# Eight-core attention and MLP block: semaphore waits on an engine's own writes, the order around a head's first value products, the place of two scalings, and a bank rotation

## The chip, the cores and the metric

The kernel runs on all eight cores of one Trainium2 chip. Each core handles half of the 128-row tiles of one of the four sequences (the cores of a pair take alternate tiles), and no core waits for another. The metric is the device time of the slowest core, in microseconds (us).

## The reference, cut to what matters

The block works on x of shape (4, 4096, 1024). A first RMS norm feeds one projection to 5120 columns: three 512-column parts of a gated short convolution, q, k and v of four attention heads, and two gates. Per head:

```python
s = einsum('bqhcd,bkhcd->bhcqk', q, k) * scale     # c = 0, 1: two softmax maps per head
s = where(dist >= 0, s - slope[h] * dist, -inf)    # ALiBi, causal
p = softmax(s);  a = p[:, :, 0] - lam * p[:, :, 1]
o = rmsnorm(einsum('bhqk,bkhv->bqhv', a, v), subln_g) * (1 - lam_init)
x = x + (g_a * (conv @ w_a_out) + g_b * (o @ w_b_out)) @ w_o
x = x + square(relu(rmsnorm(x) @ w_mlp_in)) @ w_mlp_out      # then a last rmsnorm
```

## The kernel before, in words

**Order of work.** The program is a list of operations per engine, made in one Python pass; each engine runs its own list strictly in order. `Sched._add` (L62) works out what an operation waits for: the last writers and the readers of the buffers that it names. A wait for TensorE on itself is left out; ScalarE and VectorE do wait, through a semaphore, for their own earlier writer of a buffer (L78 to L81). A write called `part` doesn't wait for earlier `part` writes of the same buffer (L68), and a later reader waits for all of them (L96). Before the change only DMAs could be `part`.

**Stages.** First some 54 us of loads and first projections. Then attention, in four groups `g` of 512 query rows, each of four heads, each head a row of pairs of key tiles (`pairs`, L681 to L686): 4, 8, 12 and 16 pairs per head, 160 in all, numbered n = 0 to 159; group 1 starts at n = 16, group 2 at 48, group 3 at 96. Last, from some 568 us on, the rest of the merge and the MLP.

**One pair.** The main loop (L1285 on) emits for pair n, while n + 1 is prepared:

1. `qk(n + 1)` (L689): four score products, into banks 0 and 1 (s = 0) and 2 and 3 (s = 1). Their left side has 64 rows, so that the two of one s run at the same time.
2. `ex(n + 1)` (L700): the exponentials on ScalarE, PSUM to the tile PT. In heads 1 to 3 it is one instruction per s. In head 0 the ALiBi bias changes at column 256, and there are two per s, both writing the same PT.
3. `work` (L1299): operations put off for later (`run_deferred`, L804: VectorE work in portions, against a credit of 2200 ns a pair), then `one_chunk` (L1238): one chunk, that is one projection of 8 (some 4) products of 512 columns into a free bank, from a list W written out in advance. During pairs this bank is always bank 7, so a chunk waits until the one before it has been copied out (evacuated) by ScalarE or VectorE. Steps of weight 0 in W (loads, statistics) run with the chunk in front of them. Inside, `flush_masks` emits the triangular mask `mask(n + 1)` (L719) on VectorE, for pairs on the diagonal; the first pair of each head is one.
4. `pv(n, 0)` and `pv(n, 1)` (L732): the value products, up to 16 of 129 columns, into banks 4 to 6.

After a head's last pair `epilogue` (L747) copies banks 4 to 6 to SBUF with three VectorE instructions (L752 twice, L755), and queues the rest (L761 to L797) as work for later; then comes one more chunk. So at the start of a head two chunks are apart by no more than `qk` of the next pair: chunk A (from the last iteration of the head before), `qk(n + 1)`, chunk B, then `pv(n, 0)`.

**Group boundaries.** At a group's last pair `until` (L1250) runs all chunks that the next group needs, with banks from a ring: (7, 0, 1, 2, 3), starting at 7. Before group 1 these are the chunk k(1, 3), the small product of `halo_norm` (L557; it takes a bank, weight 0), and four q chunks; before group 2 three v chunks of block 6; before group 3 none. Then follows `qk` of the new group, in banks 0 to 3.

**Statistics.** `stats(blk, ...)` (L501) gives five steps: four Squares on ScalarE (L488, 1024 columns with an accumulator), then `last`: `rstd`, one VectorE operation (L483) and a power on POOL (L484). For blocks 6 and 7 `last` also scales the result on VectorE (L506), which waits for POOL. `halo_stat` (L550) is a Square (L551) with its own root. `spread` (L919) deals the steps out evenly among chunks: W takes `halo_stat`, the five steps for block 1 and two loads among the four chunks `vs(5)`, which run at n = 3 to 6. `halo_chunk` (L613) is copied out by a ScalarE copy (L623) and a VectorE product (L624).

Of the kernel before, what the change touches and what calls it, by code (L numbers as in the profile page):

```python
# [36 lines left out]
class Sched:  # L37
# [66 lines left out]

    def op(self, eng, fn, reads=(), writes=()):
        return self._add(eng, fn, reads, writes, False)

# [123 lines left out]
def build_program():  # L231
# [201 lines left out]

    def act(fn, reads, writes):
        S.op("act", fn, reads, writes)

    def dve(fn, reads, writes):
        S.op("dve", fn, reads, writes)

# [61 lines left out]
    def stats(blk, nxt):  # L501

        def last():
            rstd(rs1[blk], ss1[blk], 4)
            if blk in ksc:
                dve(lambda e: e.tensor_scalar_mul(ksc[blk].ap, rs1[blk].ap, 0.125), [rs1[blk]], [ksc[blk]])  # L506

        def sq(t):
            def f():
                stat_tile(blk, t, tok[(blk, t)])  # L510
                if nxt is not None:
                    tok_load(nxt, t)
            return f
        return [sq(0), sq(1), sq(2), sq(3), last]

# [97 lines left out]
    def halo_chunk(chs):  # L613
        def f():
# [7 lines left out]
            lo, hi = chs[0], chs[-1] + 1  # L622
            act(lambda e: e.copy(hh.ap[:, lo:hi, :], v[:, :, 0, :]), ck, [hh])  # L623
            dve(lambda e: e.tensor_tensor(hh.ap[:, lo:hi, :], v[:, :, 1, :], hh.ap[:, lo:hi, :], ALU.mult),  # L624
# [75 lines left out]
    def ex(n):  # L700
        p = pairs[n]
        g, h, j, cs = p["g"], p["h"], p["j"], p["cs"]
        pts[n] = []
        for s in range(2):
            blk, t = 4 * s + j // 4, j % 4
            PT = pt_ring.next()
            pts[n].append(PT)
            col = ((j - 4 * g + 12) * 2 + s) * 5
            if h == 0:
                parts = [(a, b, col + k) for k, (a, b) in enumerate(((cs, 256), (max(cs, 256), 512))) if a < b]  # L710
            else:
                parts = [(cs, 512, col + 1 + h)]
            scale = ksc[blk].ap[:, t:t + 1] if blk in ksc else 0.125
            for a, b, c in parts:
                act(lambda e, a=a, b=b, c=c, s=s, PT=PT, scale=scale: e.activation(  # L715
                    PT.ap[:, :, a:b], Sb[s][:, :, a:b], AF.Exp, bias=ccol(C_BTAB + c), scale=scale),
                    Sk[s] + [cst] + ([ksc[blk]] if blk in ksc else []), [PT])

# [28 lines left out]
    def epilogue(g, h):  # L747
# [3 lines left out]
        def out(m):  # L751
            dve(lambda e: e.tensor_copy(o[:, m, 0:3, 0:129], bank(4 + m)[:, 0:390].rearrange(  # L752
                "p (t e) -> p t e", t=3)[:, :, 0:129]), [pk(4 + m)], [o_raw])
        out(0)
        dve(lambda e: e.tensor_copy(o[:, :, 3, 0:129], bank(6)[:, 0:260].rearrange(  # L755
            "p (m e) -> p m e", m=2)[:, :, 0:129]), [pk(6)], [o_raw])
        out(1)
# [429 lines left out]
    mark(0)  # L1187
    W += [(0, f) for f in normed(0)] + spread(ks(5)[1:], [])
    W += spread(vs(5), [halo_stat] + stats(1, 2) + wc_load(0))
    W += spread(vs(1), xT_steps(2, 2))  # L1190
# [58 lines left out]

    def until(name, banks=range(8)):  # L1250
        keep, oring[0] = oring[0], Ring(list(banks))
        while pos[0] < marks[name]:
            one_chunk(marks[name])
# [31 lines left out]
    for n, p in enumerate(pairs):  # L1285
        if n == n_a3 - 16:
            g_loads2(0)
        if n + 1 < len(pairs):
            if pairs[n + 1]["g"] != p["g"]:
                until(pairs[n + 1]["g"], (7, 0, 1, 2, 3))  # L1290
            qk(n + 1)
# [7 lines left out]
        def work(room):  # L1299
# [3 lines left out]
            one_chunk(limit)  # L1303
            flush_masks()
        if not p["last"]:
            work(2200 - (400 if diag else 0))
        pv(n, 0)
        pv(n, 1)
# [159 lines left out]
```

How the kernel before makes its waits and increments, by code:

```python
        def run(e, eng):  # L135
            seen = {}
            for i, o in enumerate(self.ops[e]):
                deps = set(o["deps"])
                if o["is_dma"]:
                    j = o["ev"][2]
                    if j >= N_DMA_SEMS:
                        deps.add(("d", e, j - N_DMA_SEMS))
                need = {}
                for d in deps:
                    s, v = sem_val(d)
                    if need.get(id(s), (s, 0))[1] < v:
                        need[id(s)] = (s, v)
                for key, (s, v) in sorted(need.items(), key=lambda kv: kv[1][1]):
                    if seen.get(key, 0) >= v:
                        continue
                    seen[key] = v
                    eng.wait_ge(s, v)
                ins = o["fn"](eng)
                if o["is_dma"]:
                    s, v = sem_val(o["ev"])
                    ins.then_inc(s, 16)
                elif i in cval[e]:
                    ins.then_inc(csem[e], 1)
            n = self.dma_count[e]
            for k in [(n + q) % N_DMA_SEMS for q in range(N_DMA_SEMS)]:
                cnt = (n - k + N_DMA_SEMS - 1) // N_DMA_SEMS if n > k else 0
                if cnt > 0:
                    eng.wait_ge(dsem[e][k], 16 * cnt)
```

## Time and profile before

| | us |
|---|---|
| median of 3 runs (lowest, highest) | 1164.12 (1163.68, 1166.56) |
| profiled execution, its own time | 1163.79 |
| its span on the slowest core (core 5) | 1162.2 |
| spans of the eight cores | 1160.2 to 1162.2 |
| granted TensorE clock, mean, of the cores | 0.995 to 0.998 |
| TensorE busy | 1127.2 (97% of the span) |
| ScalarE busy / VectorE busy | 550.3 / 466.9 |

PE is TensorE, PEld its loads of weights, ACT ScalarE, DVE VectorE, POOL GpSimd. All matrix products have line L441, so they are told apart by form and by time. The record of one product lasts from its start to its result in PSUM, while the next starts long before that; "busy" is the union of the records, and "idle before" counts only what no record covers. In the rows below, "<-" names what ended a wait.

### The profile page before, as it was taken

Reading aid. Unit: us, or ns where it says so; the run is one execution under the profiler, and the core shown is the slowest. Engines: PE = TensorE matmul, PEld = TensorE weight load, DVE = VectorE, ACT = ScalarE, POOL = GpSimd, SP = SyncE. Lnnn points to the kernel's source line nnn. Section 1 sums busy time; section 2 is a strip of 40 time slices with the busy share of each in tenths; the row PEclk is TensorE's granted clock in tenths of the full one; section 3 lists DMA queues with packets and bytes.
Section 4 is the critical chain, followed back from the end, with each engine's and each line's share of the span. In section 5 each row is a group of like instructions: output and inputs, shape, how many; then the busy total and the mean of one; then the engine's idle time right before and its main releaser. Section 6 shows DMA issues by size and latency. Waiting matters only on the chain.

```text
span 1162.2 us, 20430 instructions; the slowest of 8 cores (1160.2 to 1162.2 us)
## 1 busy us (share of the span) xinstructions
PE 1127.2 (97%) x7162; PEld 563.0 (48%) x7162; DVE 466.9 (40%) x1051; ACT 550.3 (47%) x760; POOL 84.3 (7%) x136
## 2 busy tenths in 40 slices
PE   7999999999999999999999999999999999999997
PEld 3444555455455555555544444444444444444444
DVE  2476666644654632433435544222221322223212
ACT  2585786676666888878523223321231033003301
POOL 5212001001001001001100001000000000000000
PEclk8999999999999999999999999999999999999999
DMA  9877522332067059375296686911210140012001
GB/s 140 166 144 138 144 90 51 110 56 46 5 132 147 19 99 179 65 191 105 38 253 168 207 165 172 158 43 55 70 57 1 55 111 17 19 55 73 2 37 55
DMA packets 67491, 111.46 MB, mean 96 GB/s; under 512 B 37216, under 2 KB 40288, under 8 KB 66368
## 3 DMA queue, kind: packets, MB, share of 16 engines
q0 software_dynamic: 15056, 40.22, 22.5%
q1 hardware_dynamic: 52192, 69.68, 20.0%
q8 instruction: 60, 0.98, 0.4%
q14 instruction: 39, 0.32, 0.1%
q10 hardware_dynamic: 144, 0.26, 0.1%
HBM read 114.40 MB, written 29.36 MB: 124 GB/s over the span
## 4 chain that ended last, share of the span: by engine, by line
PE 92%; ACT 3%; DVE 2%; issue 2%; DMA 1%; POOL 0%; DVEq 0%; ACTq 0%; POOLq 0%
PE ps_all L441 92%; ACT big L715 2%; DMA big<-wv 1%; DVE big L780 0%; DVE big L594 0%; DVE big L604 0%; POOL big L484 0%; ACT big L852 0%; DVE big L772 0%; DVE big L863 0%; DVE big L574 0%; ACT big L592 0%; POOL big L446 0%; DVEq L152 0%; DVE big L571 0%
## 5 line engine op out<-in xcount | busy, mean ns | idle before, releaser
L441 PE MATMUL ps_all<-big 128*128 128x512 bf16 (+7 forms) x7162 | 1127.2, 323 | 28.9 <-ACT big L715 8.2
L441 PEld LDWEIGHTS ps_all<-big 128*128 128x128 bf16 (+2 forms) x7162 | 563.0, 98 | 592.9 <-issue 100.7
L715 ACT ACTIVATE big<-ps_all,big 128x1024 bf16<-128x1024 f32 (+3 forms) x384 | 338.3, 926 | 111.4 <-PE ps_all L441 104.4
L982 ACT ACTIVATE big<-ps_all 128x512 bf16<-128x512 f32 x128 | 76.5, 598 | 137.6 <-PE ps_all L441 137.4
L983 DVE TENSOR_TENSOR big<-big 128x512 bf16<-128x512 bf16 x128 | 54.5, 426 | 156.5 <-ACT big L982 156.0
L999 ACT ACTIVATE big<-big 128x1024 bf16<-128x1024 f32 x15 | 15.9, 1057 | 187.9 <-DVE big L994 187.9
L863 DVE SCALAR_TENSOR_TENSOR big<-big,ps_all 128x512 f32<-128x512 f32 x64 | 43.7, 687 | 106.3 <-PE ps_all L441 106.3
L994 DVE SCALAR_TENSOR_TENSOR big<-ps_all,big 128x512 f32<-128x512 f32 x30 | 22.5, 752 | 143.5 <-PE ps_all L441 143.5
L852 ACT ACTIVATE big<-ps_all,big 128x512 f32<-128x512 f32 x64 | 43.6, 686 | 67.7 <-PE ps_all L441 66.6
L898 ACT ACTIVATE big<-big 128x1024 bf16<-128x1024 f32 x16 | 16.9, 1057 | 47.0 <-DVE big L893 47.0
L724 DVE TENSOR_TENSOR big<-big 128x256 bf16<-128x256 bf16 x64 | 18.5, 289 | 46.7 <-ACT big L715 46.6
L893 DVE SCALAR_TENSOR_TENSOR big<-ps_all,big 128x512 f32<-128x512 f32 x32 | 22.1, 691 | 29.2 <-PE ps_all L441 29.0
L788 POOL TENSOR_TENSOR big<-big 128x4 f32<-128x4 f32 x16 | 17.4, 1088 | 158.4 <-DVE big L786 153.6
L772 DVE SCALAR_TENSOR_TENSOR big<-big 128x128 f32<-128x128 f32 x64 | 22.4, 351 | 5.5
L867 DVE TENSOR_TENSOR big<-big 128x512 bf16<-128x512 f32 x32 | 22.2, 692 | 3.7 <-DVE big L863 0.5
L594 DVE TENSOR_SCALAR big<-ps_all,big 128x512 bf16<-128x512 f32 x18 | 13.5, 751 | 24.1 <-PE ps_all L441 24.1
L534 DVE SCALAR_TENSOR_TENSOR big<-big 128x512 bf16<-128x512 bf16 x32 | 22.7, 745 | 0.0
L446 POOL DMA_DIRECT2D big<-xT x33 | 18.4, 586 | 46.5 <-PE ps_all L441 46.4
L780 DVE SCALAR_TENSOR_TENSOR big<-big 128x128 f32<-128x128 f32 x64 | 18.7, 292 | 7.2 <-DVE big L780 0.5
L488 ACT ACTIVATE big<-big 128x1024 bf16<-128x1024 f32 x20 | 21.1, 1057 | 0.5
L752 DVE COPY big<-ps_all 128x387 f32<-128x387 f32 x32 | 17.9, 560 | 4.2 <-PE ps_all L441 2.5
L1102 ACT ACTIVATE big<-big 128x512 bf16<-128x512 bf16 x24 | 13.4, 621 | 12.4 <-DMA big<-xT 12.4
(90 smaller groups left out, 296.8 us busy)
## 6 DMA issues: line engine op xcount, KB each, us to landing
big<-xs SPq DMA_DIRECT2D x36, 512.0 KB, 6.8
big<-w POOLq DMA_DIRECT2D x32, 512.0 KB, 8.1
xm_sp<-big SPq DMA_DIRECT2D x16, 512.0 KB, 3.8
big<-xm_sp SPq DMA_DIRECT2D x16, 512.0 KB, 5.8
big<-xT POOLq DMA_DIRECT2D x31, 256.0 KB, 7.6
out<-big SPq DMA_DIRECT2D x15, 512.0 KB, 2.7
xn_sp<-big SPq DMA_DIRECT2D x4, 1024.0 KB, 6.6
big<-wg POOLq DMA_DIRECT2D x8, 512.0 KB, 5.9
```

What stands on the lines that cost most here:

```text
L441: S.op("pe", lambda e: e.matmul(out, lhsT, rhs, start=start, stop=stop, skip_group_check=skip), reads, writes)
L488: act(lambda e: e.activation(junk.ap, xt.ap, AF.Square, accum_out=ss1[blk].ap[:, t:t + 1]), [xt], [junk, ss1[blk]])
L534: dve(lambda e: e.scalar_tensor_tensor(x[k].ap, x[k].ap, ccol(C_GMIX + k), r.ap, ALU.mult, ALU.mult), [x[k], cst, r], [x[k]])
L715: act(lambda e, a=a, b=b, c=c, s=s, PT=PT, scale=scale: e.activation(PT.ap[:, :, a:b], Sb[s][:, :, a:b], AF.Exp, bias=ccol(C_BTAB + c), sc ...
L772: dve(lambda e, t=t: e.scalar_tensor_tensor(o[:, 0, t, 0:128], o[:, 0, t, 0:128], rl[:, 0, t:t + 1], o[:, 1, t, 0:128], ALU.mult, ALU.add) ...
L852: lambda ps, lo, hi, key: act(lambda e: e.activation(t.ap[:, lo:hi], ps, AF.Tanh, bias=hbg.ap[:, 8 * w + dm:8 * w + dm + 1], scale=0.5), k ...
L863: lambda ps, lo, hi, key: dve(lambda e: e.scalar_tensor_tensor(t.ap[:, lo:hi], t.ap[:, lo:hi], 1.0, ps, ALU.add, ALU.mult), key + [t], [t]))
L867: dve(lambda e: e.tensor_tensor(g_m[dm].ap, a.ap, b.ap, ALU.add), [a, b], [g_m[dm]])
L893: dve(lambda e: e.scalar_tensor_tensor(x.ap[:, o:o + 512], ps, 0.5, x.ap[:, o:o + 512], ALU.mult, ALU.add), key + [x], [x])
L982: act(lambda e: e.activation(r.ap, ps, AF.Relu), key, [r])
L983: dve(lambda e: e.tensor_tensor(h2[fc].ap, r.ap, r.ap, ALU.mult), [r], [h2[fc]])
L994: dve(lambda e: e.scalar_tensor_tensor(x.ap[:, hs], ps, r2q[b].ap[:, t:t + 1], x.ap[:, hs], ALU.mult, ALU.add), key + [x, r2q[b]], [x])
```

## The change

- `op`, `act` and `dve` get the argument `part`. The exponentials of one PT tile, and the three copies of `epilogue` into `o_raw`, become parts: the second and third no longer wait for the one before on their own engine. The mask and other readers wait for all.
- `stats` gives the scaling of blocks 6 and 7 as a sixth step of its own, `scaled`, so that `spread` deals out six steps.
- `halo_chunk`'s copy moves from ScalarE to VectorE.
- In W, the three chunks `ks(5)[1:]` and the four `vs(5)` now share the five statistics steps of block 1, `halo_stat` and the two loads, in this order.
- `until` for groups 1 to 3 takes its banks from (0, 1, 2, 3, 7), and the ring's start is set to minus the sum of the weights that are left, modulo five.
- At the first pair of every head but the very first, `pv(n, 0)` goes ahead of the chunk, and `pv(n, 1)` stays behind it.

```diff
--- before.py
+++ after.py
@@ -102,8 +102,8 @@
             self.readers.setdefault(k, []).append(ev)
         return ev
 
-    def op(self, eng, fn, reads=(), writes=()):
-        return self._add(eng, fn, reads, writes, False)
+    def op(self, eng, fn, reads=(), writes=(), part=False):
+        return self._add(eng, fn, reads, writes, False, (), part)
 
     def dma(self, eng, fn, reads=(), writes=(), extra=(), part=False):
         return self._add(eng, fn, reads, writes, True, extra, part)
@@ -431,11 +431,11 @@
             late_masks.pop(0)()
 
 
-    def act(fn, reads, writes):
-        S.op("act", fn, reads, writes)
-
-    def dve(fn, reads, writes):
-        S.op("dve", fn, reads, writes)
+    def act(fn, reads, writes, part=False):
+        S.op("act", fn, reads, writes, part)
+
+    def dve(fn, reads, writes, part=False):
+        S.op("dve", fn, reads, writes, part)
 
     def mm(out, lhsT, rhs, start, stop, reads, writes, skip=False):
         S.op("pe", lambda e: e.matmul(out, lhsT, rhs, start=start, stop=stop, skip_group_check=skip),
@@ -502,8 +502,9 @@
 
         def last():
             rstd(rs1[blk], ss1[blk], 4)
-            if blk in ksc:
-                dve(lambda e: e.tensor_scalar_mul(ksc[blk].ap, rs1[blk].ap, 0.125), [rs1[blk]], [ksc[blk]])
+
+        def scaled():
+            dve(lambda e: e.tensor_scalar_mul(ksc[blk].ap, rs1[blk].ap, 0.125), [rs1[blk]], [ksc[blk]])
 
         def sq(t):
             def f():
@@ -511,7 +512,7 @@
                 if nxt is not None:
                     tok_load(nxt, t)
             return f
-        return [sq(0), sq(1), sq(2), sq(3), last]
+        return [sq(0), sq(1), sq(2), sq(3), last] + ([scaled] if blk in ksc else [])
 
     def bcast(blk):
 
@@ -620,7 +621,7 @@
                            xnTh.ap[:, c, :], c == 0 and w == 0 and q == 0, c == 7, [Wc[ch], xnTh], ck, skip=True)
             v = pc[:, 0:64 * len(chs)].rearrange("p (q w t) -> p q w t", w=2, t=32)
             lo, hi = chs[0], chs[-1] + 1
-            act(lambda e: e.copy(hh.ap[:, lo:hi, :], v[:, :, 0, :]), ck, [hh])
+            dve(lambda e: e.tensor_copy(hh.ap[:, lo:hi, :], v[:, :, 0, :]), ck, [hh])
             dve(lambda e: e.tensor_tensor(hh.ap[:, lo:hi, :], v[:, :, 1, :], hh.ap[:, lo:hi, :], ALU.mult),
                 ck + [hh], [hh])
         return f
@@ -711,10 +712,11 @@
             else:
                 parts = [(cs, 512, col + 1 + h)]
             scale = ksc[blk].ap[:, t:t + 1] if blk in ksc else 0.125
+            S.parts.discard(PT)
             for a, b, c in parts:
                 act(lambda e, a=a, b=b, c=c, s=s, PT=PT, scale=scale: e.activation(
                     PT.ap[:, :, a:b], Sb[s][:, :, a:b], AF.Exp, bias=ccol(C_BTAB + c), scale=scale),
-                    Sk[s] + [cst] + ([ksc[blk]] if blk in ksc else []), [PT])
+                    Sk[s] + [cst] + ([ksc[blk]] if blk in ksc else []), [PT], True)
 
     def mask(n):
         p = pairs[n]
@@ -750,10 +752,11 @@
 
         def out(m):
             dve(lambda e: e.tensor_copy(o[:, m, 0:3, 0:129], bank(4 + m)[:, 0:390].rearrange(
-                "p (t e) -> p t e", t=3)[:, :, 0:129]), [pk(4 + m)], [o_raw])
+                "p (t e) -> p t e", t=3)[:, :, 0:129]), [pk(4 + m)], [o_raw], True)
+        S.parts.discard(o_raw)
         out(0)
         dve(lambda e: e.tensor_copy(o[:, :, 3, 0:129], bank(6)[:, 0:260].rearrange(
-            "p (m e) -> p m e", m=2)[:, :, 0:129]), [pk(6)], [o_raw])
+            "p (m e) -> p m e", m=2)[:, :, 0:129]), [pk(6)], [o_raw], True)
         out(1)
         rl = est.ap[:, 0:8].rearrange("p (m t) -> p m t", m=2)
 
@@ -1185,8 +1188,8 @@
     W = []
     W += [(0, f) for f in xT_steps(1, 0)] + [(1, ks(5)[0])]
     mark(0)
-    W += [(0, f) for f in normed(0)] + spread(ks(5)[1:], [])
-    W += spread(vs(5), [halo_stat] + stats(1, 2) + wc_load(0))
+    W += [(0, f) for f in normed(0)]
+    W += spread(ks(5)[1:] + vs(5), stats(1, 2) + [halo_stat] + wc_load(0))
     W += spread(vs(1), xT_steps(2, 2))
     W += [(1, bcast(1))]
     W += spread(ks(1) + qs(1), stats(2, None) + wc_load(1) + [halo_norm]
@@ -1247,8 +1250,10 @@
             pos[0] += 1
         return w
 
-    def until(name, banks=range(8)):
+    def until(name, banks=range(8), turn=False):
         keep, oring[0] = oring[0], Ring(list(banks))
+        if turn:
+            oring[0].i = -sum(w for w, f in W[pos[0]:marks[name]]) % len(banks)
         while pos[0] < marks[name]:
             one_chunk(marks[name])
             run_deferred(900)
@@ -1287,7 +1292,7 @@
             g_loads2(0)
         if n + 1 < len(pairs):
             if pairs[n + 1]["g"] != p["g"]:
-                until(pairs[n + 1]["g"], (7, 0, 1, 2, 3))
+                until(pairs[n + 1]["g"], (0, 1, 2, 3, 7), True)
             qk(n + 1)
             ex(n + 1)
             if pairs[n + 1]["first"]:
@@ -1302,9 +1307,13 @@
                 late_masks.append(lambda: mask(n + 1))
             one_chunk(limit)
             flush_masks()
+        lead = p["first"] and n > 0
+        if lead:
+            pv(n, 0)
         if not p["last"]:
             work(2200 - (400 if diag else 0))
-        pv(n, 0)
+        if not lead:
+            pv(n, 0)
         pv(n, 1)
         if p["last"]:
             epilogue(g, p["h"])
```

## Rows read from the trace of the kernel before

**Rows 1.** Windows, middle and last stage: TensorE, weight loads, VectorE, ScalarE, GpSimd busy.

```profile
54.05:567.95 513.90, 492.36 (x4114) 270.36 (x4115) 261.93 (x631) 388.31 (x480) 54.09 (x78) 1.00 0.48 99
...
567.95:1162.20 594.25, 588.17 (x2756) 269.55 (x2756) 186.91 (x372) 140.67 (x244) 11.66 (x21) 1.00 0.35 88
```

**Rows 2.** Groups by form, TensorE: count, busy us, mean ns of one record.

```profile
L441 PE MATMUL ps_all<-big 128*128 128x512 bf16 x4064 | 907.5, 380 | 14.8 <-DMA big<-xT 2.1 <-DVE big L566 2.0 <-DVE big L571 1.8
L441 PE MATMUL ps_all<-big 128*128 128x129 bf16 x2176 | 149.4, 220 | 0.7 <-DVE big L724 0.7
```

**Rows 3.** Chain of waits, last stage: start, us, what.

```profile
567.95 588.18 PE ps_all L441 x2756
```

**Rows 4.** Timeline of ScalarE, head 0 of group 2.

```profile
244.24 3.01 ACT L715 ACTIVATE big<-ps_all,big 128x512 bf16<-128x512 f32 x4 [0.38 <-PE ps_all L441]
...
254.35 1.36 ACT L715 ACTIVATE big<-ps_all,big 128x512 bf16<-128x512 f32 x2 [0.80 <-PE ps_all L441]
```

**Rows 5.** Chain of waits, first pairs of group 1, head 0.

```profile
114.44 0.79 ACT big L715
...
115.37 0.71 PE ps_all L441 x3
```

**Rows 6.** Windows: pairs 98 to 105, 62 to 69, 50 to 56, 106 to 109.

```profile
382.00:409.55 27.55, 27.14 (x228) 15.20 (x226) 14.30 (x33) 23.91 (x35) 1.83 (x2) 1.00 0.12 27
266.05:292.16 26.11, 26.11 (x226) 14.43 (x225) 8.66 (x21) 19.46 (x20) 3.23 (x5) 1.00 0.32 46
226.36:250.40 24.04, 23.84 (x198) 13.39 (x196) 11.87 (x28) 21.19 (x31) 2.37 (x4) 1.00 0.21 40
409.55:422.64 13.09, 11.73 (x106) 6.87 (x106) 2.36 (x4) 12.29 (x20) 1.05 (x2) 1.00 0.55 97
```

**Rows 7.** Timeline of TensorE at the two group boundaries.

```profile
102.53 12.38 PE L441 MATMUL ps_all<-big 128*128 128x512 bf16 x60 [0.49 <-DVE big L483]
...
213.19 5.66 PE L441 MATMUL ps_all<-big 128*128 128x512 bf16 x25 [0.55 <-DVE big L594]
219.54 2.97 PE L441 MATMUL ps_all<-big 64*128 64x512 bf16 x17 [0.69 <-DVE big L483]
```

**Rows 8.** Timeline of VectorE around the two L506.

```profile
176.28 0.17 DVE L506 TENSOR_SCALAR big<-big 128x4 f32<-128x4 f32 x1 [1.46 <-POOL big L484]
...
302.44 0.17 DVE L506 TENSOR_SCALAR big<-big 128x4 f32<-128x4 f32 x1 [1.29 <-POOL big L484]
```

**Rows 9.** Timeline of TensorE behind them.

```profile
179.62 2.57 PE L441 MATMUL ps_all<-big 128*128 128x512 bf16 x20 [1.12 <-DVE big L604]
...
305.55 3.33 PE L441 MATMUL ps_all<-big 128*128 128x512 bf16 x28 [1.01 <-DVE big L571]
```

**Rows 10.** Timeline of ScalarE, pairs 4 and 5.

```profile
67.29 1.04 ACT L551 ACTIVATE big<-big 32x1024 bf16<-32x1024 f32 x1
...
69.57 1.85 ACT L715 ACTIVATE big<-ps_all,big 128x768 bf16<-128x768 f32 x2
```

**Rows 11.** Timeline of TensorE, pairs 5 and 6.

```profile
72.14 2.57 PE L441 MATMUL ps_all<-big 128*128 128x512 bf16 x20 [0.29 <-ACT big L592]
...
75.76 0.23 PE L441 MATMUL ps_all<-big 64*128 64x128 bf16 x2 [0.44 <-ACT big L715]
```

**Rows 12.** Timeline of TensorE, start of group 1, head 3 (pair 40).

```profile
191.40 2.79 PE L441 MATMUL ps_all<-big 128*128 128x512 bf16 x24 [0.34 <-DVE big L761]
```

**Rows 13.** Timeline of VectorE at the same place.

```profile
189.65 0.56 DVE L752 COPY big<-ps_all 128x387 f32<-128x387 f32 x1
190.12 0.28 DVE L724 TENSOR_TENSOR big<-big 128x256 bf16<-128x256 bf16 x1
```

**Rows 14.** Timelines: VectorE at pair 17, TensorE at pair 59.

```profile
121.69 0.75 DVE L594 TENSOR_SCALAR big<-ps_all,big 128x512 bf16<-128x512 f32 x1
...
259.89 0.39 PE L441 MATMUL ps_all<-big 128*128 128x129 bf16 x4 [0.66 <-DVE big L724]
260.50 2.42 PE L441 MATMUL ps_all<-big 128*128 128x512 bf16 x12 [0.21 <-DVE big L525]
```

## The prediction

> **What bounds the kernel now.** I read the windows by stage first. In the last stage TensorE is busy for 588.17 of 594.25 us, and the chain of waits calls all of it one run of products; in the middle stage, from 54 to 568 us, it is busy for 492.36 of 513.90 [rows 1, 3]. The change touches only operations of the middle stage and the bank rings in front of it, so the last stage moves as a block, and the question is how much of the middle stage's waiting goes away.
>
> Idle time understates that waiting. The long run has 2756 products in 588.18 us, 0.213 us from start to start, while the record of a 512-column product lasts 0.380 [rows 2, 3]. So a product's record covers 0.165 us of any gap behind it (a value product's 0.220 record does the same: four in 0.39 us start 0.057 apart [rows 14]); behind a pair of score products, which start together, the whole 0.380 is covered where the second of the pair is late, and, by my estimate, 0.07 where a chunk follows, since it can't start at once in any case. I give each stall from start to start: idle plus that cover. The middle stage's 21.5 us idle sit in some 45 gaps, so about 29 us can be won at most, 21.5 + 45 x 0.165.
>
> **Exponentials.** Head 0 has 40 pairs, of which 32 have two exponentials per s, so 64 instructions lose their wait. Four in a row with two such waits take 3.01 us, two without one take 1.36; as one record is about 0.77, a step without a wait is 0.59 [rows 4]. Two more such steps on the 1.36 would give 2.54, so the waits cost at most 0.47 in four; scaled by a tile's column rather than by a constant an instruction is slower by some 0.09, which leaves 0.29 as the least. I take 0.19 a wait, 0.37 a pair. That is 11.9 us of ScalarE, but it counts only where TensorE waits for it:
> - In groups 1, 2 and 3 the chain runs through the first pair's exponentials to the score product that needs their bank again (pair 17's, 115.37) [rows 5]: 3 x 0.37 = 1.1. A like stall at pair 21 gives 0.4.
> - Eight pairs of group 3's head 0 took 27.55 us, eight of group 2's head 1, which have one exponential per s, 26.11, 3.26 a pair: 1.44 lost. Seven of group 2's head 0 took 24.04 against 22.85: 1.19 lost [rows 6]. Each pair's excess, 0.17, is under the 0.37 that ScalarE gets back, so nearly all goes; I take 1.2 and 1.0.
> - Pairs 106 to 109, where gates are on ScalarE too, took 13.09 us for 106 products and had 1.36 idle [rows 6]. Four pairs' 0.37 is 1.5; pairs with a chunk of four stay bound by ScalarE: 1.1.
>
> Together **4.8**. Bounds: 0 (ScalarE gets nothing back) and 6.3 (all these stalls end).
>
> **Banks.** Before group 1 the chunk k(1, 3) waited 0.49 + 0.165 = 0.66 us for bank 7, which the chunk before had just filled; before group 2 the first v chunk waited 0.55 + 0.165 = 0.72 in the same way, and then the second score product waited for bank 1, the last chunk's, 0.69 + 0.38 = 1.07 [rows 7]. With the new ring group 2's three chunks get banks 2, 3 and 7: -1.79, banks 2 and 3 being free since pair 47's small exponentials. For group 1 the weights left are k and four q, sum 5, modulo 5 nothing; but `halo_norm` also takes a bank, with weight 0. So six banks are drawn: 0, 1, 2, 3, 7, and 0 for the last q chunk, right before `qk(16)` wants bank 0. Before, the same six draws from (7, 0, 1, 2, 3) ended on 7. There the k chunk's 0.66 goes, and the wait that group 2 loses, 1.07, comes. So 1.79 + 0.66 - 1.07 = **1.4** is won. Bounds: 0.8 if the first chunks wait for exponentials in their new banks, 2.4 if no stall comes at group 1.
>
> **Roots.** L506 held VectorE for 1.46 us at block 6 and 1.29 at block 7, waiting for POOL's power; behind it stood the conv operations and the copy of bank 7, and TensorE waited 1.12 + 0.07 and 1.01 + 0.07 us [rows 8, 9]. As a step of its own the scaling comes two chunks later for block 6 and one for block 7, over 3 us, and finds POOL done. -1.19 in full; at block 7 VectorE has 2.2 us of the epilogue's work queued in front of the copy, so -0.9: **2.1**. The price is that Squares move up by a chunk; one lands before pair 28's exponentials, where TensorE waits for them: 0.27 later. Bounds 1.2 to 2.7.
>
> **Order in W, halo copy.** Between exponentials of pairs 4 and 5 ScalarE ran L551 and a Square, 2.3 us (67.29 to 69.57) [rows 10], then two more Squares before pair 6's. TensorE waited at each bank they shared: four stalls, of which two are shown, 0.37 and 0.60 by start, 1.9 in all; and 0.45 more at pair 4, 0.13 at pair 6 [rows 11]. In the new order Squares run at pairs 0 to 3, where ScalarE has time, and only one of them stands before pair 5. Left is the copy of a v chunk behind pair 5's exponentials, 0.34, and the next copy behind VectorE's epilogue work, some 0.4. So 2.5 - 0.75 = 1.75. The halo copy on VectorE frees a 0.24 wait at pair 28, which the 0.27 above takes back. **1.6**. Bounds 0.8 and 2.5.
>
> **A head's first value products.** Chunk B waits for bank 7 from chunk A, 0.34 + 0.07 = 0.42 us at pair 40 [rows 12]; the eight value products put between last 8 x 0.057 = 0.46 and cover it. They need the head's mask: it ended at 190.40, chunk B started at 191.40 [rows 12, 13], and the copies lose their own waits, so the products find it done. What is late next is chunk B itself: it is copied out 0.46 later in relation to chunk C. With 0.43 us to spare there, where VectorE is prompt, that costs 0.03. But where VectorE works its queue without a pause, as at pair 17, whose copy started with no idle before it [rows 14], the 0.46 comes back as a stall. By heads: stalls of 0.37 to 0.48 at pairs 8, 32, 40, 60, 72, 84, 144 (2.9) and of 0.16 at 48, 112 and 128 (0.5) go; given back are 0.46 at 12, 0.44 at 16, 0.36 at 40, 0.42 at 144 (ScalarE is late there whatever comes), 0.22 at 8, and small ones, together 2.0. **1.4**. Bounds: -1.5 and 3.4.
>
> **Own waits of VectorE's copies.** Two consecutive copies without a wait overlap: the mask started 0.09 before the second L752 ended (190.12 against 190.21), while a waited one starts some 0.1 after [rows 13]. So some 0.2 to 0.4 us of VectorE a head, off the path except as room for the mask: nothing.
>
> The Trainium skill (VectorE: DVE Perf Modes, "The DRAIN you can't avoid") says that chained operations can't save by dropping semaphores, since the next one doesn't start until the pipe is empty, and that the semaphore costs nothing extra. By that rule the copies gain nothing, which doesn't touch the sum; taken for ScalarE as well it would take 4.8 out. The rows show an overlap where no wait stands, on both engines, so the measurement decides against it here.
>
> **Sum.** 4.8 + 1.4 + 2.1 + 1.6 + 1.4 = 11.3. The profiled execution's own time is 1163.79, 0.33 under the median of the runs, so 1163.79 - 11.3 = **1152.5**.
>
> **Rivals.**
> 1. *The waits cost nothing, or the change doesn't take them away* (another buffer of the same instruction still orders them). For: the span of an instruction hardly tells pipe from wait. Against: rows 4. The 4.8 is gone: 1157.3. Chance 0.08.
> 2. *VectorE's queue eats the head starts.* Each start gives back 0.25 us instead of gaining: 1152.5 + 1.4 + 15 x 0.25 = 1157.7. For: pair 17. Against: most evacuations had idle time before them. Chance 0.1.
> 3. *The ring is right in every group*, if the small product's bank is free early or its draw doesn't count: 1152.5 - 1.07 = 1151.4. Chance 0.12.
> 4. *Slower.* TensorE is in order, so a value product that stands before the chunk blocks it. If VectorE's queue makes the mask late, as at pair 59, where the products waited 0.66 + 0.07 us and the chunk behind them 0.21 + 0.165 more [rows 14], each of 15 starts stalls by these 1.1. It decides from (11.3 - 1.4) / 15 = 0.66 us a start; at 1.1 the time is 1163.8 - 9.9 + 16.5 = 1170.4. Against: 1.0 us in hand at pair 40. Chance 0.03.
> 5. *1 and 2 together*: 1162.5, no change. Chance 0.05.
>
> The forecast has 0.62. About 0.3% (3.5 us) is what a measurement can tell from no change. **Range** 1148.5 to 1158.0: it holds rivals 1 to 3; the lower end is 4 us of the 6 that the upper bounds allow beyond the sum, the upper one leaves out 4, 5 and the lowest bounds taken together. Faster by over 0.3%: 0.91; within: 0.06; slower: 0.03.
>
> **What would show it.** Second exponentials start 0.1 before the one before ends, and eight pairs of head 0 take some 26.3 us. At group 1 a score product waits about 1 us for the copy of a q chunk, at group 2 none. L506 has no idle before it. At heads' first pairs value products come right behind the scores, without idle before them, and stalls of chunk C or D show at pairs 12, 16 and 40. The middle stage takes 502.6 us instead of 513.9; the last stage is unchanged. Wrong would be: a longer last stage, head 0 at its old pace, or idle time before first value products.

## The result, and the profile after

The changed kernel took 1150.99 us (median of 4 runs) against 1164.05 for the kernel before: a ratio of 0.9882, interval 0.9863 to 0.9902, some 13 us faster. One of its four runs took 1224.45 us, with the cores of one die at a lower granted clock (0.915 to 0.939), and all ratios here leave such runs out. The forecast was 1152.5, range 1148.5 to 1158.0. The profiled execution's own time is 1150.69, its span 1149.1 us on core 7.

The time went where it was looked for. Windows by stage, changed kernel (columns as in [rows 1]):

```profile
53.32:554.38 501.06, 488.65 (x4114) 268.61 (x4115) 259.75 (x633) 381.67 (x477) 53.65 (x78) 1.00 0.52 102
554.38:1149.10 594.72, 588.33 (x2756) 269.50 (x2756) 186.62 (x372) 140.43 (x244) 11.65 (x21) 1.00 0.34 88
```

The middle stage went from 513.90 us [rows 1] to 501.06, that is 12.8 less (502.6 had been forecast), and TensorE's idle time in it from 21.5 to 12.4. The last stage, forecast unchanged, is 0.47 us longer on this core. The chain of waits shows one new break in what was a single piece [rows 3]:

```profile
554.38 45.28 PE ps_all L441 x209
...
599.71 0.19 ACT big L901
599.90 0.58 ACT big L855
...
600.62 542.43 PE ps_all L441 x2544
```

A gate's activation by ScalarE (L855), which empties a bank, came behind the accumulator read of a Square (L901). The forecast's "unchanged" holds on three of the six cores whose product records are complete (594.20 to 594.28 us) and misses by 0.3 to 0.7 on the other three, while all six of the kernel before lie at 594.23 to 594.27. Whether the break belongs to the change isn't shown.

**Exponentials.** Windows of pairs 98 to 105, 62 to 69, 50 to 56 and 106 to 109 (answering to [rows 6]):

```profile
370.63:396.95 26.32, 26.29 (x227) 14.73 (x226) 14.70 (x34) 22.49 (x35) 1.83 (x2) 1.00 0.14 26
257.11:283.22 26.11, 26.11 (x226) 14.43 (x224) 9.08 (x22) 20.50 (x22) 3.23 (x5) 1.00 0.37 47
219.22:242.26 23.04, 23.01 (x198) 13.03 (x197) 12.38 (x29) 19.89 (x32) 2.42 (x4) 1.00 0.23 41
396.95:409.01 12.06, 11.60 (x106) 6.65 (x104) 2.36 (x4) 11.49 (x19) 1.05 (x2) 1.00 0.64 104
```

Eight pairs of head 0 take 26.32 us (27.55 before; "some 26.3 us" forecast) and keep up with a head that has one exponential per s, which is as it was at 26.11; seven pairs take 23.04 (24.04), and the four with gates 12.06 (13.09). ScalarE's timeline at the same head as [rows 4]:

```profile
236.22 2.60 ACT L717 ACTIVATE big<-ps_all,big 128x512 bf16<-128x512 f32 x4 [0.67 <-PE ps_all L441]
...
245.86 1.36 ACT L717 ACTIVATE big<-ps_all,big 128x512 bf16<-128x512 f32 x2 [0.96 <-PE ps_all L441]
```

Four exponentials take 2.60 us instead of 3.01, so a wait on the own engine cost 0.205 (0.19 was taken), and two that never had one still take 1.36. ScalarE now waits 0.67 us for TensorE before that row (0.38 before the change), and TensorE has no more than 0.03 us idle in the eight pairs.

**Group boundaries.** TensorE at groups 1 and 2 (answering to [rows 7]), and VectorE before group 1:

```profile
109.58 2.99 PE L441 MATMUL ps_all<-big 64*128 64x512 bf16 x18 [0.95 <-DVE big L605]
112.83 3.46 PE L441 MATMUL ps_all<-big 64*128 64x512 bf16 x28 [0.27 <-ACT big L717]
...
211.72 7.46 PE L441 MATMUL ps_all<-big 128*128 128x512 bf16 x47
```

```profile
108.74 0.69 DVE L605 TENSOR_TENSOR big<-ps_all,big 128x512 bf16<-128x512 f32 x1 [0.38 <-PE ps_all L441]
```

Before group 2 nothing waits any more. Before group 1 the score product of pair 16 waits 0.95 us idle for L605, the copy of the last q chunk: the weight-0 draw of `halo_norm` has put it into bank 0, as forecast ("about 1 us").

**Roots and head starts.** VectorE's two scalings, then TensorE around pairs 36 and 40 and VectorE at pair 40 (answering to [rows 8, 9, 12, 13]):

```profile
171.36 0.16 DVE L507 TENSOR_SCALAR big<-big 128x4 f32<-128x4 f32 x1
...
292.05 0.16 DVE L507 TENSOR_SCALAR big<-big 128x4 f32<-128x4 f32 x1
```

```profile
167.78 8.40 PE L441 MATMUL ps_all<-big 128*128 128x129 bf16 x69
...
183.87 8.35 PE L441 MATMUL ps_all<-big 128*128 128x129 bf16 x61
```

```profile
185.19 0.28 DVE L726 TENSOR_TENSOR big<-big 128x256 bf16<-128x256 bf16 x1
```

Neither scaling has idle time before it, and at the two places where TensorE waited 1.12 and 0.34 us it now runs through. The mask of pair 40 ended at 185.47, in the middle of that run, before its value products.

**What is left.** TensorE's stalls behind head starts:

```profile
97.22 2.99 PE L441 MATMUL ps_all<-big 128*128 128x512 bf16 x19 [0.66 <-DVE big L575]
120.50 2.68 PE L441 MATMUL ps_all<-big 128*128 128x512 bf16 x22 [0.65 <-DVE big L595]
299.08 1.24 PE L441 MATMUL ps_all<-big 128*128 128x512 bf16 x5 [0.59 <-DVE big L572]
```

These are stalls of a later chunk, such as the prediction expected at heads 12, 16 and 40, where VectorE works its queue without a pause: chunks 14 and 18 wait, the one expected behind head 40 doesn't, and chunk 74, behind head 72, does.

### The profile page after: what moved, and what is told of

It reads as the page before. It is cut to its first block, busy times and chain, and to the rows that moved or that the text cites. A ratio compares the mean times of both kernels' runs of the same rounds, so it can differ in the third digit from the quotient of the medians.

```text
span 1149.1 us, 20398 instructions; the slowest of 8 cores (1147.2 to 1149.1 us)
## 1 busy us (share of the span) xinstructions
PE 1122.7 (98%) x7162; PEld 560.4 (49%) x7162; DVE 464.4 (40%) x1053; ACT 544.2 (47%) x758; POOL 83.8 (7%) x136
## 4 chain that ended last, share of the span: by engine, by line
PE 93%; ACT 2%; DVE 1%; DMA 1%; issue 1%; POOL 0%; DVEq 0%; ACTq 0%; POOLq 0%
PE ps_all L441 93%; ACT big L717 1%; DMA big<-wv 1%; POOL big L446 0%; DVE big L783 0%; DVE big L866 0%; DVE big L775 0%; ACT big L593 0%; DVE big L605 0%; DVE big L575 0%; ACT big L855 0%; DVE big L595 0%; DVE big L758 0%; DVE big L572 0%; DVE big L731 0%
## 5 line engine op out<-in xcount | busy, mean ns | idle before, releaser
L717 ACT ACTIVATE big<-ps_all,big 128x1024 bf16<-128x1024 f32 (+3 forms) x384 | 331.7, 927 | 103.5 <-PE ps_all L441 102.1
L866 DVE SCALAR_TENSOR_TENSOR big<-big,ps_all 128x512 f32<-128x512 f32 x64 | 43.7, 686 | 106.2 <-PE ps_all L441 106.0
L855 ACT ACTIVATE big<-ps_all,big 128x512 f32<-128x512 f32 x64 | 43.6, 686 | 68.0 <-PE ps_all L441 65.7
L901 ACT ACTIVATE big<-big 128x1024 bf16<-128x1024 f32 x16 | 16.9, 1057 | 47.9 <-DVE big L896 47.9
L726 DVE TENSOR_TENSOR big<-big 128x256 bf16<-128x256 bf16 x64 | 18.4, 288 | 44.4 <-ACT big L717 44.3
L791 POOL TENSOR_TENSOR big<-big 128x4 f32<-128x4 f32 x16 | 17.4, 1088 | 135.1 <-DVE big L789 130.9
L446 POOL DMA_DIRECT2D big<-xT x33 | 18.5, 596 | 43.9 <-PE ps_all L441 43.8
L1063 DVE SCALAR_TENSOR_TENSOR big<-big 128x1024 f32<-128x1024 f32 x15 | 19.1, 1276 | 0.0
```

The costliest lines, as they stand in the source:

```text
L855: lambda ps, lo, hi, key: act(lambda e: e.activation(t.ap[:, lo:hi], ps, AF.Tanh, bias=hbg.ap[:, 8 * w + dm:8 * w + dm + 1], scale=0.5), k ...
L866: lambda ps, lo, hi, key: dve(lambda e: e.scalar_tensor_tensor(t.ap[:, lo:hi], t.ap[:, lo:hi], 1.0, ps, ALU.add, ALU.mult), key + [t], [t]))
```

## The experiments

From here on the middle stage is the measure: the time from its first product to the first of the last stage, on core 7 of each profiled execution. (Two of the eight cores lack some records of products and are left out throughout.) Over the six cores of two executions of the changed kernel it lies between 500.69 and 501.23, while the stage ahead of it took 52.2 to 55.5 us without regard to the kernel. "By the starts of the score products" means: the score products come in the same order in every kernel, so the start of each, counted from the stage's first product, is set against its start in the other kernel, and where the difference jumps the time was lost or won. A jump at pair n + 2 belongs to chunk n or the products beside it. The ratio is that of the timed runs.

| kernel | middle stage, us | against its base | ratio to before (interval) |
|---|---|---|---|
| before | 513.92 | | |
| changed | 501.06 | -12.86 | 0.9882 (0.9863, 0.9902) |
| changed, again | 501.05 | -12.87 | 0.9892 (0.9875, 0.9909) |
| without exponentials' part | 506.98 | +5.92 | 0.9942 (0.9924, 0.9959) |
| before + exponentials' part | 508.90 | -5.02 | 0.9958 (0.9943, 0.9973) |
| without roots | 503.44 | +2.38 | 0.9906 (0.9888, 0.9924) |
| without order and halo copy | 503.65 | +2.59 | 0.9914 (0.9890, 0.9938) |
| old ring | 502.15 | +1.09 | 0.9898 (0.9880, 0.9916) |
| without head starts | 502.17 | +1.11 | 0.9902 (0.9886, 0.9918) |
| before + head starts | 513.11 | -0.81 | 0.9991 (0.9981, 1.0000) |
| copies wait again | 501.33 | +0.27 | 0.9889 (0.9872, 0.9907) |
| ring of six at group 1 | 499.82 | -1.24 | 0.9875 (0.9851, 0.9899) |
| the same, no head start at 12, 16 | 499.22 | -1.84 | 0.9879 (0.9862, 0.9896) |
| ring of six, less room | 501.67 | +0.61 | 0.9887 (0.9869, 0.9905) |

One thing must be taken off first. The cores of the changed kernel differ in two places above all: 0.16 us at pair 122 and 0.11 at pair 125. In its first execution cores 1, 3, 5 and 7 have both and take 501.06 to 501.23; in both executions the cores with neither take 500.69 to 500.81. No row says what these two stalls wait for. Core 7 of the first execution, the base of the third column, has both. On core 7 of the other rows only "changed, again" and the last have one, the 0.16. So, like with like, the whole change is worth 13.1, each undone part 0.27 more than the column says, and the ring of six 0.27 less.

**1. Exponentials, undone and alone.** First the changed kernel with the exponentials waiting again:

```diff
-                    Sk[s] + [cst] + (...), [PT], True)
+                    Sk[s] + [cst] + (...), [PT])
```

> The changed kernel, but the exponentials of a tile wait for their own engine again. My theory: the 0.19 us a wait come back on ScalarE and the 4.8 us of the sum come back, 1151.0 + 4.8 = 1155.8; from pair 98's to pair 106's first score product the time goes from some 26.4 us to 27.5, the stall of pair 49's score product grows by 0.37. Rival 1 (a wait for the own engine costs nothing): 1151.0, with the pace of the changed kernel. Rival 2 (the gain lies in the order around a head's start): 1151.0 as well.

Then the kernel before with only that part:

> The kernel before with the exponentials' change alone. My theory: 4.8 us less, 1159.2, less what the second wait at the same place takes back: pair 18's chunk waits for VectorE at the same moment as for ScalarE, so pair 19's 0.35 stays. Rival 1: 1164.0. If the gain needs the other parts: 1162 to 1163.

The windows of pairs 98 to 105 (first without the part in the changed kernel, then with it in the kernel before):

```profile
374.93:402.76 27.83, 27.15 (x226) 15.20 (x226) 14.71 (x34) 23.91 (x35) 1.83 (x2) 1.00 0.10 22
```

```profile
380.70:407.01 26.31, 26.27 (x226) 14.71 (x225) 14.39 (x33) 22.49 (x35) 1.83 (x2) 1.00 0.14 27
```

ScalarE's 1.42 us in eight pairs (23.91 less 22.49) come and go with the waits, and the eight pairs get longer or shorter by as much: 1.51 in the changed kernel, 1.24 in the one before. Rival 1 is out. Alone the part is worth 5.0, in company 6.2 (5.9 and the 0.27): by the starts of the score products, 0.3 of the difference lies at pairs 17 to 20 and 0.27 in pairs 98 to 105, where TensorE waited longer for ScalarE once other waits were gone, and 0.28 each at pairs 29 and 149. Those two are in heads with one exponential per s, which the edit doesn't touch; at 29 a score product waits for ScalarE, but why it is later there stays open.

**2. Roots, undone.**

```diff
             rstd(rs1[blk], ss1[blk], 4)
+            if blk in ksc:
+                scaled()
...
-        return [sq(0), sq(1), sq(2), sq(3), last] + ([scaled] if blk in ksc else [])
+        return [sq(0), sq(1), sq(2), sq(3), last]
```

> The changed kernel with the scaling by 1/8 of the roots of blocks 6 and 7 again in the step of the root itself, so that VectorE waits for POOL there. My theory: 2.1 us come back, 1153.1: L506's wait of some 1.3 to 1.5 us on VectorE returns twice, and with it TensorE's 1.19 at pair 36 and 0.9 at pairs 73 and 74. Rival (other work fills the place, as TensorE's own time is the bound): 1151.0 with the wait on VectorE but no stall on TensorE.

TensorE at pairs 36 and 73, roots undone:

```profile
177.65 4.52 PE L441 MATMUL ps_all<-big 128*128 128x512 bf16 x34 [0.93 <-DVE big L607]
...
299.11 3.33 PE L441 MATMUL ps_all<-big 128*128 128x512 bf16 x28 [1.41 <-DVE big L574]
```

Both stalls are back, 0.99 and 1.46 us by the starts of the score products, with 0.17 more at pair 35. Between the kernel before and the changed one the same two places gave 1.17 and 1.06.

**3. Order in W and halo copy, undone.**

```diff
-            dve(lambda e: e.tensor_copy(hh.ap[:, lo:hi, :], v[:, :, 0, :]), ck, [hh])
+            act(lambda e: e.copy(hh.ap[:, lo:hi, :], v[:, :, 0, :]), ck, [hh])
...
-    W += [(0, f) for f in normed(0)]
-    W += spread(ks(5)[1:] + vs(5), stats(1, 2) + [halo_stat] + wc_load(0))
+    W += [(0, f) for f in normed(0)] + spread(ks(5)[1:], [])
+    W += spread(vs(5), [halo_stat] + stats(1, 2) + wc_load(0))
```

> The changed kernel with the old order of the statistics among the chunks of block 5 and the halo copy on ScalarE again. My theory: 1.6 us come back; the four stalls at pairs 5 to 7 (0.47, 0.37, 0.45, 0.60) return, less what the products ahead of the chunk cover, and 0.24 at pairs 24 and 28. Rival (ScalarE has room enough once the rest is changed): no difference.

TensorE at pairs 5 and 6, then at pairs 24 and 28, both undone (core 5):

```profile
72.01 0.28 PE L441 MATMUL ps_all<-big 64*128 64x256 bf16 x2 [0.60 <-ACT big L717]
72.59 2.57 PE L441 MATMUL ps_all<-big 128*128 128x512 bf16 x20 [0.29 <-ACT big L593]
75.53 0.23 PE L441 MATMUL ps_all<-big 64*128 64x128 bf16 x2 [0.38 <-ACT big L717]
76.20 0.23 PE L441 MATMUL ps_all<-big 64*128 64x128 bf16 x2 [0.43 <-ACT big L717]
...
141.94 11.98 PE L441 MATMUL ps_all<-big 128*128 128x129 bf16 x134 [0.30 <-DVE big L764]
154.69 1.67 PE L441 MATMUL ps_all<-big 128*128 128x512 bf16 x7 [0.16 <-DVE big L625]
```

The changed kernel has at pairs 5 to 7 one stall of 0.15 (the v chunk's copy behind pair 5's exponentials) and one of 0.30, and at pairs 24 and 28 neither of the other two. There the halo copy (L624), behind the exponentials on ScalarE, held VectorE's product with it (L625). VectorE before the first of the two (core 5):

```profile
141.37 0.23 DVE L625 TENSOR_TENSOR big<-ps_all,big 128x64 f32<-128x64 f32 x1 [1.06 <-ACT big L624]
141.51 0.28 DVE L726 TENSOR_TENSOR big<-big 128x256 bf16<-128x256 bf16 x1
```

Behind L625 stood the mask of pair 24 (L726), which ended at 141.79, 0.15 us before the value products that the head start puts there; at pair 28 the chunk waits for L625 itself, for bank 7. (The row of TensorE names L764, a small operation behind the mask; the epilogue's copies had ended a microsecond before L625 began.) By the starts of the score products the undone order loses 1.97 us up to pair 8, 0.57 at pairs 26 to 30, and 0.29 at pair 140, whose cause wasn't looked into. Of the 0.36 at pair 26 some 0.2 comes only with head starts: between the kernel before and the changed one that place gave 0.16, and head starts alone in the kernel before lose 0.20 there, in the same wait for the mask. So the halo copy is worth 0.37 by itself (0.16 and 0.21), and more once value products come first. (This kernel's ratio rests on two runs.)

**4. The ring.** The changed kernel with the old ring:

```diff
-                until(pairs[n + 1]["g"], (0, 1, 2, 3, 7), True)
+                until(pairs[n + 1]["g"], (7, 0, 1, 2, 3))
```

> The changed kernel with the old ring (7, 0, 1, 2, 3), starting at 7. My theory: before group 1 the chunk k(1, 3) waits again for bank 7 (0.66 us by start) while the last q chunk gets bank 7, so the score product of pair 16 no longer waits for its copy (the changed kernel's stall of 1.0 goes); before group 2 the first v chunk waits 0.72 and the second score product 1.07. Middle stage 501.0 + 0.66 + 0.72 + 1.07 - 1.0 = 502.4 us. Rival A (the new ring gives nothing at group 1's chunk, since what stood behind the stall absorbs it later): 502.4 - 0.66 = 501.8. Rival B (the stalls of the new ring at group 1 are as large as all those of the old one): 501.0.

```profile
100.75 13.60 PE L441 MATMUL ps_all<-big 128*128 128x512 bf16 x71 [0.49 <-DVE big L483]
...
215.01 2.97 PE L441 MATMUL ps_all<-big 64*128 64x512 bf16 x17 [0.69 <-DVE big L483]
```

The stalls of [rows 7] are back, and no score product waits at pair 16. By the starts of the score products the new ring loses 0.35 us at group 1 and wins 1.68 at group 2, 1.4 together; the 1.1 of the table has the 0.27 of pairs 122 and 125 taken off.

So at group 1 I gave the ring six banks in the order that the six draws need:

```diff
+                if pairs[n + 1]["g"] == 1:
+                    until(1, (3, 0, 1, 2, 3, 7))
+                else:
+                    until(pairs[n + 1]["g"], (0, 1, 2, 3, 7), True)
```

> The changed kernel with six banks for the six draws before group 1, (3, 0, 1, 2, 3, 7), so that neither the k chunk nor pair 16's first score product finds its bank full. My theory: the stall of 1.01 us before pair 16's scores goes and nothing comes in its place, since the chain from there through the exponentials to pair 17's starts earlier as a whole: 1.0 us less than the changed kernel. Rival 3 (the ring costs nothing there): no difference. A second rival: the chain has another end, VectorE's queue behind pair 15, and only 0.3 to 0.5 is won.

> The changed kernel once more, unedited, as the one to compare the others of this job with on their chip. Both theories: the ratio to the kernel before as measured first, 0.988, some 13 us less; the middle stage as in its first trace. What differs between its two traces is what a single trace can't tell.

The stall of 0.95 is gone, 1.01 us by the starts of the score products, and the middle stage is 1.24 shorter with the 0.27. Three runs took 1150.09 to 1150.39 us, against 1151.68 to 1152.72 for the changed kernel on the same chip.

**5. Head starts.** Undone, then alone in the kernel before:

```diff
-        lead = p["first"] and n > 0
+        lead = False
```

> The changed kernel with a head's first value products behind the chunk again, all else kept. My theory: 1.4 us come back, 1152.4: seven stalls of some 0.42 us before chunk B return (pairs 8, 32, 40, 60, 72, 84, 144), and those behind pairs 12 and 16 (0.24 and 0.63 at pairs 13 and 14, 0.72 at pair 18) get smaller by 0.46 and 0.44. Rival 2 (VectorE's queue eats the starts): the order costs 3.75 us, so without it 1147.2. If the starts gain in full: 3.4 come back, 1154.4.

> The kernel before, with nothing of the change but the first value products ahead of the chunk. My theory: the gain is that of the changed kernel without its other parts, 0.7 to 1.4 us: a middle stage of 513.9 - 1.1 = 512.8. Rival A (the copies' own waits make the mask late where value products come first): 15 starts lose 0.2 to 0.4 us each, so 513.9 - 1.1 + 4 = 516 or more. Rival B (in the kernel before other stalls take the gain back): 513.9.

TensorE at pair 40, head starts undone:

```profile
187.01 6.07 PE L441 MATMUL ps_all<-big 128*128 128x512 bf16 x52 [0.34 <-DVE big L764]
```

The stall of [rows 12] is back as it was. Summed over the places where the two kernels' score products drift apart, the head starts win 3.8 us (up to 0.45 at a head) and give back 2.4: 0.40, 0.21 and 0.45 behind heads 4, 8 and 12, 0.45 at chunk 18, 0.43 at chunk 74, and at head 144 the 0.39 that was won there. That is 1.4 us net, which the table has as 1.1 for the 0.27. In the kernel before they are worth 0.8 on core 7, and 0.46 to 0.57 on cores 0, 1 and 3.

Without them at heads 12 and 16 alone, and with the ring of six:

> The same with the value products of pairs 12 and 16 behind the chunk again, where VectorE works without a pause. My theory: 0.46 and 0.44 us more, together 1.9 us less than the changed kernel; the stalls of chunks 13, 14 (0.24, 0.63) shrink to 0 and 0.4 and that of chunk 18 from 0.72 to some 0.3. Rival (these stalls come from Squares on ScalarE or the late mask, not from the order): as ring6.

Another 0.6 us in the middle stage, so at these two heads they cost more than they win. The timed runs don't tell: 1149.57 to 1151.77 us, against 1150.09 to 1150.39 with the ring of six alone.

**6. The copies' own waits.**

```diff
-                "p (t e) -> p t e", t=3)[:, :, 0:129]), [pk(4 + m)], [o_raw], True)
+                "p (t e) -> p t e", t=3)[:, :, 0:129]), [pk(4 + m)], [o_raw])
```

(and the same for bank 6.)

> The changed kernel, but the second and third copy into o_raw wait again for the one before on VectorE. My theory: each wait costs VectorE some 0.2 us, 0.4 a head, and the mask ends 0.4 us later; it still ends before the value products at most heads, so the middle stage stays at 501.0, within 0.15 us. Rival (with value products ahead of the chunk the mask is on the path at every head): up to 14 x 0.2 to 0.4 us, the middle stage 503.8 or more.

VectorE at the epilogue before pair 72, first the changed kernel, then with the waits:

```profile
289.33 0.56 DVE L754 COPY big<-ps_all 128x387 f32<-128x387 f32 x1
289.80 0.42 DVE L758 COPY big<-ps_all 128x258 f32<-128x258 f32 x1
290.13 0.55 DVE L754 COPY big<-ps_all 128x387 f32<-128x387 f32 x1
290.60 0.28 DVE L726 TENSOR_TENSOR big<-big 128x256 bf16<-128x256 bf16 x1
```

```profile
290.73 0.56 DVE L754 COPY big<-ps_all 128x387 f32<-128x387 f32 x1
291.45 0.43 DVE L758 COPY big<-ps_all 128x258 f32<-128x258 f32 x1 [0.17 <-PE ps_all L441]
291.98 0.56 DVE L754 COPY big<-ps_all 128x387 f32<-128x387 f32 x1
292.46 0.28 DVE L726 TENSOR_TENSOR big<-big 128x256 bf16<-128x256 bf16 x1
```

From the first copy to the mask it is 1.27 us without the waits and 1.73 with them. (The row of the second copy names TensorE for its idle 0.17, so a part of the first gap may be TensorE's.) Two losses stay: chunk 74, which already waited for VectorE, waited 0.35 us longer, and 0.19 lies at pair 94, where TensorE's rows show no gap. The middle stage is 501.33 to 501.38 us on the four cores that have neither of the stalls at pairs 122 and 125, some 0.6 more than the changed kernel's 500.69 to 500.81: more than the 0.15 of my theory, far from the rival's 2.8.

**7. Why chunks wait behind head starts.** The kernel of experiment 4, with less put-off work let out in a head's second pair:

```diff
-            work(2200 - (400 if diag else 0))
+            work(2200 - (400 if diag else 0) - (1000 if n > 5 and pairs[n - 1]["first"] else 0))
```

> The changed kernel with the six-bank ring (3, 0, 1, 2, 3, 7) at the group boundaries, and with 1000 ns less of put-off VectorE work let out in the second pair of each head. My theory: the stalls that are left at the second chunk behind a head's first value products (pairs 13, 14, 18, 74; 0.2 to 0.7 us each) come from VectorE's queue, which copies bank 7 late; with less in front of the copies some 0.8 us goes, a middle stage of 499.85 - 0.8 = 499.0. Rival A (VectorE's work is late for another reason, or the work cut there makes a later copy or epilogue late by as much): 499.85, or up to 1 us more.

TensorE at pairs 13, 17, 74 and 115 (core 5):

```profile
95.03 5.17 PE L441 MATMUL ps_all<-big 128*128 128x512 bf16 x40 [0.17 <-DVE big L575]
...
115.84 5.34 PE L441 MATMUL ps_all<-big 64*128 64x512 bf16 x37
...
295.71 5.53 PE L441 MATMUL ps_all<-big 128*128 128x512 bf16 x51
...
425.96 2.25 PE L441 MATMUL ps_all<-big 128*128 128x512 bf16 x22 [1.01 <-DVE big L866]
```

The cause was right: the stalls of 0.66, 0.65 and 0.59 at chunks 14, 18 and 74 are gone, 1.9 us by the starts of the score products. The sum was wrong: 0.46 comes back at pairs 30 to 38, and in group 3 the chunks in the fourth pair of heads 1, 2 and 3 now wait 1.1 us each. GpSimd and VectorE ahead of the first of these:

```profile
421.30 0.53 POOL L446 DMA_DIRECT2D big<-wo  x1 [4.02 <-PE ps_all L441]
422.77 0.53 POOL L446 DMA_DIRECT2D big<-w  x1 [0.95 <-PE ps_all L441]
423.31 1.03 POOL L791 TENSOR_TENSOR big<-big 128x4 f32<-128x4 f32 x1
```

```profile
421.12 0.17 DVE L789 TENSOR_SCALAR big<-big 128x4 f32<-128x4 f32 x1
424.52 0.69 DVE L796 TENSOR_TENSOR big<-big 128x512 bf16<-128x512 f32 x1 [3.23 <-POOL big L791]
425.13 0.68 DVE L866 SCALAR_TENSOR_TENSOR big<-big,ps_all 128x512 f32<-128x512 f32 x1
```

The power L791 came a pair later in the lists and so stood behind two weight loads (L446) on GpSimd, the second of which waits 0.95 us for TensorE to give its buffer free. L796 held VectorE for it, 3.23 us, and behind L796 stood L866, the copy that the chunk's bank needs. With the full room (experiment 4) the power ran ahead of both loads, L796 waited 1.35 us instead, and the chunk didn't wait. Less room in groups 0 to 2 alone wasn't tried; by the same steps, up to pair 76, an estimate is 499.82 less 1.46, some 498.4 us for the middle stage.

## Why the prediction was right, and where it was off

| term | forecast | undone, table above | undone, like with like | bounds |
|---|---|---|---|---|
| exponentials | 4.8 | 5.9 (5.0 alone) | 6.2 | 0 to 6.3 |
| banks | 1.4 | 1.1 | 1.4 | 0.8 to 2.4 |
| roots | 2.1 | 2.4 | 2.7 | 1.2 to 2.7 |
| order, halo copy | 1.6 | 2.6 | 2.9 | 0.8 to 2.5 |
| head starts | 1.4 | 1.1 (0.8 alone) | 1.4 | -1.5 to 3.4 |
| copies' waits | 0 | 0.3 | 0.5 | |

The mechanism was right in the five terms that the sum counts, and two of them were sized right; the copies were put at nothing and are worth half a microsecond. The undone parts add up to 15.0 where the whole change gave 13.1, so 1.9 us is counted more than once. I find 1.7 of it: 1.1 that the exponentials are worth only in company, 0.4 at block 7's root (1.46 undone, 1.06 between before and changed) and the 0.2 at pair 24. Against the forecast of 11.3:

- **Exponentials.** The wait was sized right (0.205 against 0.19) and so were the places: the first pairs of groups 1 to 3 gave 0.41 each (0.37 forecast), pair 21 gave 0.4, pairs 98 to 105 1.23 (1.2), pairs 50 to 56 1.0 (1.0), 106 to 109 1.03 (1.1). With pairs 57 and 58 (0.3 more) and what is lost at pairs 18 to 20 (0.3) that makes 5.0 alone. What the sum left out is that other parts, by ending waits of TensorE's, make ScalarE the later one at pairs 17 to 20 and 98 to 105 (0.6 together); the 0.28 each at pairs 29 and 149 stay open.
- **Banks.** The three effects, 0.66 and 1.79 won and 1.07 lost, came out as a loss of 0.35 at group 1 and a gain of 1.68 at group 2. That `halo_norm`'s draw turns group 1's ring wrong was the point that decided; rival 3 would have been right only with the ring of six, which gives 1.01 us where the rival has 1.07.
- **Roots.** 1.17 at block 6 as forecast. At block 7 I took 0.2 off because VectorE has a queue in front of the copy; 1.06 came, and 1.46 goes when the part is undone. No stall of 0.27 from earlier Squares showed at pair 28.
- **Order and halo copy** is the term that was mis-sized by the largest share: 1.3 us (1.0 by the table), beyond its bound. Its own steps, 1.75 + 0.24 - 0.27, make 1.7 and not 1.6. The stalls up to pair 8 gave 1.97 (1.75 forecast). The step that failed is the last one, that the halo copy frees 0.24 us "which the 0.27 above takes back": with the copy on ScalarE, pairs 26 to 30 lose 0.57 through VectorE, 0.2 of it through the mask of pair 24, and in the changed kernel no Square takes anything back. The 0.29 at pair 140 stays open.
- **Head starts.** 3.8 won and 2.4 given back (3.4 and 2.0 forecast), so the net is right and a part of that is luck: heads 8, 12 and 16 gave back what was forecast (0.21, 0.45 and 0.45) and the 0.36 at 40 wasn't given back, but head 4 gave back 0.40 and chunk 74 0.43, which the forecast doesn't name. The 0.4 at 144 was won and given back in one pair, as forecast. Rival 2 named the right cause, and experiment 7 shows it, but at a few heads, not all. Rival 4 is seen at pairs 59 and 95 alone:

```profile
251.40 0.39 PE L441 MATMUL ps_all<-big 128*128 128x129 bf16 x4 [0.66 <-DVE big L726]
...
365.16 3.02 PE L441 MATMUL ps_all<-big 128*128 128x129 bf16 x18 [0.25 <-DVE big L726]
```

Both are last pairs of a head, which the change doesn't touch; at first pairs of the changed kernel the mask was never late. It was, by 0.3 us at pair 24, in the two kernels that have head starts and the halo copy on ScalarE (experiment 3), so rival 4's cause is real, and the move of the halo copy is what keeps it out.

- **Copies.** "Off the path" was too quick: where VectorE is the late one, its 0.4 us at an epilogue come out at a later chunk, here chunk 74 (0.35). The 0.19 at pair 94 stays open.

## What to carry to other kernels

A semaphore wait for the own engine's earlier write of another part of a buffer cost about 0.2 us each time here, on ScalarE and VectorE, and it is worth removing where that engine sets the pace; read the pace from windows over equal stretches, not from idle time. Before moving or delaying an operation, list what stands in front of it and behind it on every queue that it or its consumers use: a power let out one pair later fell behind two loads on GpSimd, started 2.0 us after its input was there, and made a chunk wait 1.1 us, through VectorE. Before reading a difference of 0.3 us from one core, look at the others: here two stalls that come and go made up 0.27 of it. A bank ring needs the count of its draws, also those of weight zero, and the last draw must miss the bank that is wanted first.

## What the runs showed of the hardware

- Two exponentials of 128x512 elements start 0.57 to 0.59 us apart without a wait between them and 0.78 with one (constant scale; 0.66 to 0.68 and 0.86 to 0.87 with a scale per row), while one's record mostly lasts 0.68 to 0.78. The Trainium skill (ScalarE: Activation LUTs, "What ACT_TABLE_LOAD costs") says that back-to-back activations overlap by about 93 ns; 0.687 less 0.59 is the same here, and the wait costs the overlap and 0.09 again.
- VectorE's copies behave alike: 1.27 against 1.73 us for three copies, of which two waited. The Trainium skill's statement that the semaphore costs nothing extra (VectorE: DVE Perf Modes, "The DRAIN you can't avoid") differs from these rows, and the measurement decides.
- The first stage took 52.2 to 55.5 us by core and execution, whatever the kernel, while the middle stage, 500 us long, repeats within 0.6 over the six cores of two executions (501.06 and 501.05 on the same one), and within 0.3 once the two stalls of pairs 122 and 125 are taken off. Effects of half a microsecond can be read in the stage where they would be lost in the total.
